# One gather stream for all ten tiles, taken in turns inside the prompt's phases

## The reference

```python
h = rmsnorm(x, g_mix)
proj = h @ w_in                       # q, k, v of both attentions, and the gates
oa = window_attention(rope(qa), rope(ka), va, sink)   # 16 heads, 3 blocks of keys
ob = dense_attention(rope(norm(qb)), rope(norm(kb)), vb)  # 8 heads, all keys
x  = x + (sig(gA) * (oa @ w_oa) + sig(gB) * (ob @ w_ob)) @ w_out
h  = rmsnorm(x, g_ffn)
# experts: 8 heads, each top 16 of 128x128 expert pairs
idx, g = top16_product_keys(h @ w_query, sub_keys), softmax(best)
act = gelu(sum(expert_u[idx] * h, -1))
x  = x + sum((g * act) * expert_v[idx])   # 128 rows of 2 x 1024 per token
return rmsnorm(x, g_final)
```

## Time and profile before

| | before |
|---|---|
| median of 3 runs | 5359.83 us (5359.02 to 5369.11) |
| the profiled execution | 5371.16 us, its span 5369.2 us |
| PE / DVE / ACT / POOL busy | 3188.3 / 3411.1 / 1014.0 / 1780.0 us |
| DMA | 1558.80 MB, of which 1342.26 MB gathers; mean 290 GB/s |
| sample's phases | 0 to 573 us |
| prompt: projection | 573 to 1200 us (matmuls from 622) |
| prompt: keys and attention | 1200 to 2010 us |
| prompt: merge | 2010 to 2410 us |
| prompt: experts | 2410 to 5369 us (sums from 2488) |

### The profile page before, as it was taken

One profiled execution on the slowest core, in us unless ns is written; L12 is line 12 of the kernel. 1 busy time (PEld: TensorE's weight loads), 2 busy tenths in 40 slices (PEclk: granted clock), 3 DMA queues, 4 the chain that ended last, 5 costly groups with the idle time before them and its releaser, 6 DMA issues.

```text
span 5369.2 us, 77195 instructions
## 1 busy us (share of the span) xinstructions
PE 3188.3 (59%) x27092; PEld 1839.0 (34%) x27092; DVE 3411.1 (64%) x7794; ACT 1014.0 (19%) x2743; POOL 1780.0 (33%) x1424
## 2 busy tenths in 40 slices
PE   8676488862888878974544445545445445454333
PEld 6436376652666653433212212212112122121000
DVE  4517666666877774657775766757757667567544
ACT  3310211101444441111111111121121111211111
POOL 0200122232434222322444434434434444344443
PEclk9787699985999999986656656656656567566555
DMA  5142477774333337666999989999989999999998
GB/s 206 52 167 87 171 296 299 290 296 147 113 132 113 132 134 309 266 231 266 388 388 377 385 350 399 389 356 383 383 354 386 388 365 389 351 388 382 377 396 332
DMA packets 270598, 1558.80 MB, mean 290 GB/s; under 512 B 27040, under 2 KB 37280, under 8 KB 102048
## 3 DMA queue, kind: packets, MB, share of 16 engines
q0 software_dynamic: 184320, 1342.26, 64.0%
q1 hardware_dynamic: 85920, 211.83, 10.6%
HBM read 1505.49 MB, written 48.50 MB: 289 GB/s over the span
## 4 chain that ended last, share of the span: by engine, by line
DMA 26%; issue 11%; PE 7%; DVE 6%; ACT 2%; POOL 2%; another core or an unknown queue 1%; DVEq 0%; POOLq 0%; ACTq 0%; SPq 0%
DMA prompt_exp_ring<-in_experts_dram,prompt_exp_idx 23%; PE prompt_exp_acc L1722 6%; DMA prompt_exp_ring<-in_experts_dram,prompt_exp_idx_all 4%; DVE prompt_exp_junk L1631 2%; POOL prompt_exp_ring L1386 2%; ACT prompt_exp_diag L1465 1%; DVE prompt_exp_best L1508 1%; PE prompt_exp_qp L1738 1%; DVE prompt_exp_pos L1512 0%; DVE prompt_exp_sel L1559 0%; DVE prompt_exp_crest L1517 0%; DVE prompt_exp_dot L1631 0%; ACT prompt_exp_ysq L1483 0%; PE prompt_exp_qp L1683 0%
## 5 line engine op out<-in xcount | busy, mean ns | idle before, releaser
L1722 PE MATMUL prompt_exp_acc<-prompt_exp_ring,prompt_exp_diag 32*32 32x512 f32 x16384 | 940.7, 946 | 1519.6 <-ACT prompt_exp_diag L1465 1491.6
L1631 DVE CUSTOM_DVE_ANT_0 prompt_exp_junk<-prompt_exp_ring,prompt_exp_h_now 128x1024 bf16<-128x1024 f32 x1024 | 1242.4, 1226 | 730.2 <-DMA prompt_exp_ring<-in_experts_dram,prompt_exp_idx 641.4
L1386 POOL DMA_INDIRECT prompt_exp_ring<-in_experts_dram,prompt_exp_idx x896 | 1049.6, 1171 | 1459.4 <-PE prompt_exp_acc L1722 1272.4
L1722 PEld LDWEIGHTS prompt_exp_acc<-prompt_exp_ring,prompt_exp_diag 32*32 32x32 f32 x16384 | 170.8, 128 | 2071.0 <-issue 2069.1
L1459 ACT ACTIVATE prompt_exp_ge<-prompt_exp_dot 128x2 f32<-128x2 f32 x512 | 104.1, 203 | 2410.8 <-DVE prompt_exp_dot L1631 2396.5
L169 DVE CUSTOM_DVE_ANT_0 bg_junk<-bg_ring,bg_h 128x1024 bf16<-128x1024 f32 x256 | 347.8, 1370 | 226.6 <-DMA bg_ring<-in_experts_dram,bg_idx 94.9
L144 POOL DMA_INDIRECT bg_ring<-in_experts_dram,bg_idx x128 | 155.3, 1213 | 714.2 <-DVE bg_acc L180 406.8
L1683 PEld LDWEIGHTS prompt_exp_qp<-prompt_exp_hT,prompt_exp_wq 128*128 128x128 f32 x2048 | 312.6, 242 | 149.9 <-issue 146.3
L180 DVE SCALAR_TENSOR_TENSOR bg_acc<-bg_ring,bg_w,bg_acc 128x1024 f32<-128x1024 f32 x256 | 346.9, 1355 | 9.1
L144 POOL DMA_INDIRECT bg_ring<-in_experts_dram,bg_window x128 | 136.4, 1066 | 630.2 <-DVE bg_acc L180 597.0
L1683 PE MATMUL prompt_exp_qp<-prompt_exp_hT,prompt_exp_wq 128*128 128x128 f32 x2048 | 337.5, 333 | 6.6 <-issue 3.4
(11 more groups left out here) (331 smaller groups left out, 5160.6 us busy)
## 6 DMA issues: line engine op xcount, KB each, us to landing
sample_proj_w<-in_w_all_dram SPq DMA_DIRECT2D x10, 2048.0 KB, 8.0
prompt_proj_w<-in_w_all_dram SPq DMA_DIRECT2D x10, 2048.0 KB
proj_dram<-prompt_proj_stage SPq DMA_DIRECT2D x80, 256.0 KB
prompt_exp_ring<-in_experts_dram,prompt_exp_idx POOLq DMA_INDIRECT x896
sample_exp_wq<-in_w_query_dram SPq DMA_DIRECT2D x4, 2048.0 KB, 18.2
prompt_att_q<-proj_dram SPq DMA_DIRECT2D x16, 512.0 KB, 11.2
mixed_dram<-prompt_att_OT SPq DMA_DIRECT2D x8, 1024.0 KB, 10.1
prompt_mrg_mixT<-mixed_dram SPq DMA_DIRECT2D x8, 1024.0 KB, 9.0
```

The costliest lines, as they stand in the source:

```text
L1386: nc.gpsimd.indirect_dma_start(out=ring[:, s % RING, :], out_offset=None, in_=experts, in_offset=bass.IndirectOffsetOnAxis(ap=column(s), a ...
L1631: nc.vector.tensor_tensor_reduce(out=junk[:, s % 2, :], in0=ring[:, s % RING, 0:D], in1=h_now[:], scale=1.0, scalar=0.0, op0=ALU.mult, op1 ...
L1722: last = nc.tensor.matmul(acc[at:at + Q, rows, :], diag[k, (g - 1) % 2, c, :], ring[k, s % RING, D + half * 512:D + half * 512 + 512], sta ...
```

## The change

`Background` is replaced by `Stream`, which holds all ten tiles' gathers, 640 pairs in one sequence with one ring of 6 slots (3 pairs). `phase_experts` is split: its choosing part becomes `phase_query`, which writes h, idx and g of every tile to DRAM, for both requests; its gathering part is `Stream`, in the form with dots on DVE, diagonals on ACT and sums on PE. Work on a pair is a "turn" of DVE, ACT and PE, and every prompt phase calls turns at fixed places of its own lists of instructions (`Share.at` spreads the number of turns over the places). POOL has only the stream.

The prompt's attention, merge and query run in groups of 1, 2, 2 and 3 tiles, each group attend, merge, query in turn, so that the stream gets the next tiles. The turns are: projection 8 (norm part) and 72; keys 8; then attend, merge, query 14, 8, 18; 28, 12, 24; 48, 28, 48; 60, 28, 44. That is 448; the other 192 pairs (three tiles) run alone in `phase_rest`. The key phase is one phase of its own that stores its results to DRAM; each group's attend loads its part. Every phase ends with barriers and frees its semaphores.

To make room for the stream's four PSUM banks, attention has 2, 1 and 1 banks for S, tb and Op in place of 4, 2 and 2, and merge has one bank for each of its tiles. RoPE of q and the gate's bias move from POOL to DVE; the squares of the keys move from POOL to ACT. The gelu of a pair runs in its turn, so in attention it stands between the exponentials. After a tile's last pair, the turn in which PE unfolds the tile's sums makes no sum of a pair, and the next turn makes two. The projection keeps one buffer of w and one of w_lo. All loops over tiles are written out. The core of the diff:

```diff
-class Background:
-    RING = 4
+class Stream:
+    RING = 6
+    BACK = RING // PAIR
+    PAIRS = NT * STEPS
+    LAST = PAIRS + 41
+    def gather(self, pool):
+        g = self.gathered
+        self.gathered += 1
+        t, k = divmod(g, STEPS)
...
+        if g >= self.BACK:
+            pool.wait_ge(self.used, g - self.BACK + 1)
+        for c in range(PAIR):
+            s = PAIR * g + c
             self.nc.gpsimd.indirect_dma_start(
+                out=self.ring[:, s % self.RING, :], out_offset=None, in_=self.experts,
...
+    def dve(self, dve):
+        nc, g = self.nc, self.dve_n
...
+        if 1 <= g <= self.PAIRS:
+            dve.wait_ge(self.gelued, q + 1)
+            nc.vector.tensor_tensor(self.wgt[:, c], self.ge[:, c], self.g[:, t % 2, c], ALU.mult).then_inc(self.weighted, 1)
+        if g < self.PAIRS:
...
+            for c in range(PAIR):
+                s, col = PAIR * g + c, PAIR * k + c
+                dve.wait_ge(self.row_ld[s % self.RING], 16 * (s // self.RING + 1))
+                nc.vector.tensor_tensor_reduce(
+                    out=self.junk[:, s % 2, :], in0=self.ring[:, s % self.RING, 0:D], in1=self.h[:, t % 2, :], scale=1.0,
...
+    def act(self, act):
+        if done and k == 1:
+            act.wait_ge(self.used, STEPS * done)
+            nc.scalar.copy(self.parts[:], self.acc[:]).then_inc(self.parts_ready, 1)
+        if g < self.PAIRS:
+            act.wait_ge(self.dotted, PAIR * (g + 1))
+            nc.scalar.activation(self.ge[:, c], self.dot[:, c], ACT.Gelu).then_inc(self.gelued, 1)
+        if 1 <= g <= self.PAIRS:
+            q = g - 1
+            act.wait_ge(self.weighted, g)
+            if q >= 2:
+                act.wait_ge(self.used, q - 1)
+            for c in range(PAIR):
+                last = nc.scalar.activation(self.diag[:, q % 2, c, :], self.fold[:], ACT.Copy, scale=self.wgt[:, col:col + 1])
+            last.then_inc(self.diag_ready, 1)
+    def pe(self, pe):
+        if done and k == 1:
+            pe.wait_ge(self.parts_ready, done)
...
+            return
+        if done and k == 2:
+            pe.wait_ge(self.y_ready, done)
+            if g - 2 < self.PAIRS:
+                self.sum_pair(pe, g - 2)
+        if 1 <= g <= self.PAIRS:
+            self.sum_pair(pe, g - 1)
...
+def phase_attend(nc, tag, nt, t0, G, proj, rope, masks, sink, q_norm_g, ident_d, state_d, mixed, bg=None, turns=0):
+        SB, TB, OB = (2, 1, 1) if bg else (4, 2, 2)
+        S, tb, Op = m.ps("S", [P, SB * 512]), m.ps("tb", [P, TB, 512]), m.ps("Op", [P, OB, 512])
+        share = Share(turns, G * NH)
...
+                        elif stage == "spread":
+                            move(act, nc.scalar.copy, 0, p_moves(i, k))
+                            if share.at(head + k):
+                                bg.act(act)
...
+    request(False, None, (0, 0), 0, [(0, ST, 0, 0, 0)])
+        request(True, bg, (8, 72), 8, [(0, 1, 14, 8, 18), (1, 2, 28, 12, 24), (3, 2, 48, 28, 48), (5, 3, 60, 28, 44)])
+        phase_rest(nc, bg)
```

More of the change, by code:

```diff
@@ L45, in __call__ @@
         self.n += 1
[L46 to L65, removed]
+        self.eng.wait_ge(self.sem, self.n)
 class Mem:
@@ L988, in _, with free, moved, turn @@
-                pairs(pe, pair)
-def phase_merge(nc, sems, tag, nt, x, mixed, proj, b_gate, w_oa, w_ob, w_out, ident_d, x2, bg=None, x2_sample=None, out=None):
+                def free(u):
+                    if u >= TB:
+                        pe.wait_ge(t_free[(u - TB) % 2], (u - TB) // 2 + 1)
+                def moved(u):
+                    pe.wait_ge(t_free[u % 2], u // 2 + 1)
+                def turn(place):
+                    if share.at(place):
+                        bg.pe(pe)
@@ new lines, in phase_merge @@
+        mix_ld, gate_ld = ([m.sem(f"{n}{b}") for b in range(MB)] for n in ("mix_ld", "gate_ld"))
+        biased, gated, y_full, y_free = (m.sem(n) for n in ("biased", "gated", "y_full", "y_free"))
+        merged_ready, m_transposed, mT_ready = m.sem("merged_ready"), m.sem("m_transposed"), m.sem("mT_ready")
+        z_full, res_ready, res_stored, chain = m.sem("z_full"), m.sem("res_ready"), m.sem("res_stored"), m.sem("chain")
+        PER = 14
+        share = Share(turns, PER * G)
+        end = bg.dve_n + turns if bg else 0
@@ L1124, in spread, with turn @@
-                def spread(n, b):
-                    act.wait_ge(m_transposed, n(1 + 1))
-                    nc.scalar.copy(mT[:], tb[:]).then_inc(mT_ready, 1)
-                    if bg:
-                        if n.base < nt - 1:
-                            bg.gelu(act, before(At(n.i, 2, n.base + 1)), 2)
-                        for k in (0, 2):
-                            bg.gelu(act, after(n), k)
-                order(act, sigmoid, spread)
-                if bg:
-                    bg.square_root(act, 1)
+                def turn(i, place):
+                    if share.at(PER * i + place):
+                        bg.act(act)
@@ L1184, in _, with turn @@
             @block.tensor
             def _(pe):
-                pe.sem_inc(m_transposed, 1)
-                def branches(n, b):
-                    pe.wait_ge(ld[b], n.i * 32 + 32 * (n.base // 2 + 1))
-                    pe.wait_ge(y_free, n(1))
+                def turn(place):
+                    if place >= 0 and share.at(place):
+                        bg.pe(pe)
+                for i in range(G):
+                    at = PER * i
+                    pe.wait_ge(mix_ld[i % MB], 16 * (i // MB + 1))
@@ L1324, in phase_experts @@
+        act_chain, chain = m.sem("act_chain"), m.sem("chain")
+        PER = 3 * HEADS
+        share = Share(turns, PER * G)
+        end = bg.dve_n + turns if bg else 0
+        NH = G * HEADS
         with nc.Block() as block:
@@ L1742, in _, with turn @@
-                tiles(pe, first, tile)
+                def turn(place):
+                    if share.at(place):
+                        bg.pe(pe)
+                pe.wait_ge(ident_ld, 16)
+                transpose_h(0)
+                for n in range(2):
+                    query(n, 0)
+                    query(n, 1)
+                pe.wait_ge(const_ld, 32)
+                scores(0)
+                for n in range(NH):
+                    i, h = divmod(n, HEADS)
+                    if n + 1 < NH:
+                        scores(n + 1)
+                    if h == HEADS - 2 and i + 1 < G:
+                        transpose_h(i + 1)
+                    if n + 2 < NH:
+                        query(n + 2, 0)
+                    turn(3 * n)
+                    if n + 2 < NH:
+                        query(n + 2, 1)
+                    turn(3 * n + 1)
+                    turn(3 * n + 2)
```

2203 lines of the change are left out of this document (965 added, 1238 removed).

## The result

The changed kernel takes 6493.5 us (median of 4 runs, 6481.1 to 6505.0); the kernel before took 5364.5 us beside it. The ratio is 1.210, 95% interval 1.207 to 1.213: 21% slower, as forecast in sign, and 173 us above the 6320 predicted. The profiled execution took 6505.0 us, span 6503.1.

What follows compares the result with a forecast made beforehand. The prediction took the experts stage to stand at the DMA rate, 5.4 us a pair. Phase terms, with turns at 7.2 us, summed to 6330 us of span, 6320 for the median; range 5550 to 6850 for 8 in 10.

Steps and rivals of the forecast that it cites:

- step 1: Stream's round: ring of three pairs moves two a round, 7.2 us a turn (6.85 to 8.05) instead of 5.4.
- step 2: Each phase with its turns: no turn faster than 7.2 us in sequence, nor than the phase's own work beside it.
- The nine tile ends: Nine times a tile's sums are copied out and PE makes no sum in one turn: 72 us.
- the full ring after pauses: After a pause the ring is full, sparing about 5 us at 16 places: -80 us.
- The signs named ahead: DMA share near 0.75, round of 14.5 us, attention about 210 us a tile, 250 to 300 table loads, query 7.2 us a part.
- Attention: Attention phases: windowed head with a turn 7.2 us, dense head with a turn 10.0; 1702 us (before 685).
- Merge: Merge phases: product groups of 7.03 us, turns over their places, 30 for each of four starts; 690 us (before 400).
- Query: Query phases: DVE 65 us a tile and 2.9 us a turn, or 7.2 a turn; 1119 us with starts.
- Last stretch: Three tiles of the stream alone: 192 turns at 7.2 us, 1382, and 25 for the last tile's end: 1407 us.
- The stream at the DMA rate: Rival: stream keeps 5.4 us a turn, each phase held by its own engine; 5660 us, chance 20%.
- Table loads on the path: Rival: ACT's table loads in attention's 150 turns stand in the round, 385 us more, about 6700; chance 11%.
- Everything under the DMA: Rival: turns fill only idle time, prompt phases take what their bytes take; 4720 us, chance 7%.

Runs made afterwards that it cites:

- run 3: Kernel before the change with its experts stage's ring of four pairs cut to two: 9643.7 us, ratio 1.801.
- run 2: Changed kernel with each pair's sum in its own turn and the ring cut from three pairs to two: 6603.3 us, ratio 1.234.
- run 1: Changed kernel with weight, diagonals and sum of pair g made in turn g instead of g+1: 5836.2 us, ratio 1.089.
- run 10: Kernel before the change with weight, diagonals and sum of pair g in step g instead of g+1, ring kept: 5204.9 us, ratio 0.972.
- Run 8: Changed kernel with every gather fetching rows of half the bytes (the wrong rows), same instruction count: 5869.3 us, ratio 1.096.
- run 4: Changed kernel with no turn inside any phase, all 640 pairs in the last stretch: 8060.2 us, ratio 1.504.
- run 7: Changed kernel with the stream's gelu replaced by a copy that needs no table: 6469.3 us, ratio 1.207.
- run 9: Changed kernel with each pair's sum in its own turn and three groups of 2, 3 and 3 tiles: 5786.7 us, ratio 1.081.

## Why the prediction was right

**The round (step 1) was right in mechanism and in sum.** The number of pairs that a round moves puts the runs in order, whatever the ring:

- one pair: 14.0 us a pair (run 3)
- two pairs: 7.24 us (the changed kernel) and 7.36 (run 2: 5655 matmuls, 176.7 pairs, in 1300 us)
- three pairs: 5.51 us (run 1: 181.5 pairs in 1000 us) and 5.33 to 5.38 (before, inside a tile)
- four pairs: 5.09 to 5.14 us (run 10, inside a tile), and 4.99 in the round shown.

The first two are 14.0 to 14.7 us over the number; from three on the landing stretches. In run 1's chain from 4800 to 5800 us it takes 56.7% of the time, 9.4 us of each round of 16.5. One of them:

```profile
5194.64 9.83 DMA bg_ring<-in_experts_dram,bg_idx
```

Within the round two terms erred against each other, and that the sum still came out is luck. I took 5.3 us beside the landing and 9.2 for it; they are 6.7 and 7.8.

Most of the first error is PE's sum, 2.16 us and not 1.3. The kernel before shows both values within 50 us of its chain: 1.30 us at 2535.82, and 2.16 at 2583.91. The windows around these two sums, columns as in the earlier trace rows:

```profile
2535.00:2538.00 3.00, 1.15 (x32) 0.27 (x32) 1.41 (x5) 0.88 (x4) 0.90 (x2) 1.00 1.01 415
2583.00:2587.00 4.00, 2.02 (x32) 0.32 (x32) 1.49 (x5) 0.63 (x3) 1.07 (x2) 0.50 0.99 358
```

The granted clock was 1.00 (2.4 GHz) at the one and 0.50 (1.2 GHz) at the other, and I had read off the fast one. In the last stretch of the changed kernel the clock stands at 0.50, so every sum is of the slow kind; before, it was 0.61 on average in the experts stage. The second error is the landing, 7.8 us where the projection had 9.2 with as many pairs in flight. There stores and weights use the DMA engines too; whether that is why, no run tests.

The Trainium skill (DMA: Bandwidth & Descriptors, Anatomy of one DMA) gives 2.0 us and the bytes at 436 GB/s. Run 8 comes near its slope: 1.05 MB less for a pair took 2.4 us off the landing, some 440 GB/s, or 2.5 us off the round, 416 GB/s. The fixed part doesn't fit: of 7.8 us the issue takes 0.94 and the bytes of two rows 4.8, less the 1.24 by which the first row is ahead; 3.3 us remain where the rule has 2.0, and the turn is 7.24 where it gave 5.9.

**The phases (step 2), term by term** (predicted, measured): sample 600, 593; norm part 78, 87; projection 602, 625; keys 140, 113; attention 1702, 1669; merge 690, 784; query 1119, 1181; last stretch 1407, 1451. The nine tile ends (+72) and the full ring after pauses (-80) lie in these; no run shows either of them by itself, and they nearly cancel in my sum. The differences are +173, the whole miss of the span. The signs named ahead were there too: a DMA share of 0.77, a round of 14.5 us, 267 table loads in attention, 473 / 2 = 237 us a tile there against about 210; only query with 48 turns took 8.2 us a part, not 7.2.

- *Attention* came out within 2%: 168, 176, 226 and 205 us a tile after a start of 20, where I had 175, 175, 228 and 207. It was built as a chain of dense heads and turns of 7.2 in the windowed ones; run 4 splits it otherwise: 120 us a tile of its own, and 4.2 us for a turn. Before run 4 I put the own time at 1290 us, and it was 1034: that my sum comes within 2% is in part luck.
- *Merge* is the largest miss, +94. Its own time was right (446 measured; by my items 8 x 42 + 4 x 30 = 456); the turn was mis-sized: 4.4 us net, where I had 234 / 76 = 3.1. I let the groups with 28 turns take 7.2 us a turn and a start; they took 266 and 268 us, which less a start of 22 is 8.7 a turn. A turn there stands in PE's list between product groups. PEclk was 0.76 to 0.87 in the four merges, and 0.86 to 0.93 in those of run 4; how much of the 94 us is the clock was not measured apart.
- *Query*, +62: the turns were right (3.6 us by both), the own time wasn't. I took 65 us a tile; run 4 shows 71 (247 - 176) to 77 (176 - 99), and a start of about 22.
- *Last stretch*, +44: 192 x 7.24 is 1390. The first matmul of its sums starts 16 us into the stretch and the last one 29 us before the end; for all that I had 25.

**The rivals.** The stream at the DMA rate (20%) was tried by run 1: with the round shortened the whole comes to 5836, where that rival had 5660. Its condition, landings within 5.5 us, is met only with half the bytes. Table loads on the path (11%): 24 us, not 385. The warning of the Trainium skill (ScalarE: Activation LUTs, Table sets: the hidden batching unit) is true of the count, 267 loads in attention, but hardly of the time here. A gelu's load mostly runs before its dots are there (1453.23 to 1454.51 us, the gelu at 1456.25). The load behind it does hold an exponential back (1456.89 to 1458.17, the exponential at 1458.19), and run 7 shows that next to nothing of this reaches the time. Everything under the DMA (7%): the phases would have had to be below 3709 us after the sample; they took 4459.

**Where the 1129 us went.** Run 4 lets the difference of the profiled spans, 6503 - 5369 = 1134 us, be split:

- The phases' own time, +856: without any turn the prompt's phases take 2771 us (591 to 3362), where those before took 1915 (573 to 2488), though these had 128 pairs of gathers among them. Attention is 1034 us against 685, and query 698 against the 78 that were not hidden under the gathers. Merge is 446 against 400; norm part with projection (514 against 627) and keys (79 against 125) are shorter, without their pairs.
- The gathers, +260: 1690 us net inside the phases and 1451 at the end, 3141 together, against 2881 in the experts stage before.
- The sample, +18.

So the larger part is not the stream's pace but what the phases cost in groups, with the buffers that they are left. The order of run 1 is a thing of its own: it gives 657 us back in the changed kernel (58% of the 1129), but 145 also in the kernel before (run 10). With the order mended in both, the change still costs 5836 - 5205 = 631 us. Of the own time run 9 shows 50 us for one group more or less. What the single buffers of attention cost by themselves was not tried, since the stream's sums hold their PSUM banks as long as it lives, so how the 856 us split into buffers, RoPE on DVE, starts and lists in order stays open.

**One step of the argument was wrong.** "So this stage stands at the DMA rate" is what I read from a share of 0.95 and 388 GB/s. Run 10 falsifies it: the round of 16.09 us over three pairs and the queue's rate lay side by side, and it was the round that held, with 7% behind it (389 against 417 GB/s inside a tile). The share gave no warning of that: inside a tile it was 0.99 before and 1.01 after the edit. It didn't touch the forecast of this change; it would have hidden the edit that pays.

## What to carry to other kernels

For a ring that is filled by transfers and freed by the last of several engines, write down the round (landing, every engine's step, the next issue) and count how many slots one round really moves: an instruction that stands behind the next slot's wait in an in-order list costs a whole slot. Before a ring is cut to make room, look for such a lag; in the changed kernel it made a third pair of slots (2.1 MB of SBUF) useless in the stretch alone, and taking it out of the kernel before gave 2.8% for nothing. Background turns inside other phases pay when their net cost there is below their cost at the end (2.5 to 4.4 us against 7.3 here), but the phases must first be costed with the groups and the buffers that the stream leaves them: here that alone was 856 us.

## What the runs showed of the hardware

- A DMA share of 0.95, or of 0.98 to 0.99 inside a tile, was not the limit: at 389 GB/s there, the same stage reached 415 and 417 GB/s (share 1.01) with one more pair in flight.
- A gather's landing depends on what is in flight: 7.8 us with two pairs moving in a round, 9.7 to 10.7 with three, 9.4 on average with three in run 1's last stretch, 12.6 with four; 5.4 us with two and half the bytes.
- 267 table loads of 1.283 us, 343 us of ACT's time, cost at most some 24 us in attention whose ACT waits for data (run 7).
- PE's sums of a pair take 2.16 us at a granted clock of 0.50 against 1.30 at 1.00, in the same kernel within 50 us.
